# A token-major value projection ahead of the convolution, its first loads in pairs

## Chip, core and metric

The kernel runs on one core of a Trainium2 chip. The metric is the device time of the core in microseconds, from the start of the program to its end; lower is better.

## What is computed

Two transformer-like blocks on 512 tokens of width 1024, float32. Only the start of the first concerns the change:

```python
def first_block(x, norm_mix_g, w_in, ...):
    h = rms_norm(x, norm_mix_g[l])
    p = h @ w_in[l]
    q_a, k_a, v_a, o_a, i_a, f_a, q_b, k_b, v_b, g_a, g_b = jnp.split(p, split_idx, axis=-1)
    qk_a = jax.nn.silu(causal_conv(jnp.concatenate([q_a, k_a], axis=-1), conv_w[l]))
    ...
    h_a = mlstm_chunkwise(q_a..., k_a..., v_a..., i_pre, f_pre)
```

`rms_norm` divides each token's row by the root of its mean square and multiplies by a gain per column. After it come a mixer with decaying memory (the part "a"), a stick-breaking attention ("b"), gates, an output projection, a feed-forward part, and the second block with three attention branches.

## The kernel before, in words

The program is written by hand, engine by engine: each engine's list of instructions is in program order and semaphores join them. There is no scheduler. The order of the work is the order of the calls in the blocks `sync`, `tensor`, `scalar`, `vector` and `gpsimd`.

**Slabs.** Every projection is a sequence of weight slabs of 1 MB, numbered in the list `slabs` (lines 396 to 452): either 1024 rows by 256 columns ("narrow", 1 KB rows), or half the rows by 512 columns ("wide", 2 KB rows, two slabs for a full column block). The first are N_QA (four narrow slabs, kind "conv", for q_a and k_a), N_IF (one half-width slab, input and forget gates), N_VA (two column blocks, so four wide slabs, kind "va"), N_QB and so on. Slab n uses buffer n % 2 of `w_raw`, `w_hi`, `w_lo`. SP loads it (`load_slab`) once the split of the slab before it in that buffer is done. ACT rounds it (`split_hi`, L602), DVE takes the remainder (`split_lo`, L610), and TensorE makes three products for each tile and k: hi with hi, hi with lo, lo with hi (L633, and `mm_half`, L656, for wide slabs). The activations are split in the same way into `act_hi` and `act_lo`.

**Feature-major and token-major.** A "conv" or "if" tile has features on the partitions and all 512 tokens in the free dimension, so it needs all tokens' activations before its first product. A "va" tile has 128 tokens on the partitions and 512 columns: it needs only that block of 128 tokens. Each tile is 24 products of 128x128 by 512, into one PSUM bank. Feature-major tiles alternate between the two banks of `ps_g`; a wide block uses two banks of `ps_z` and both of `ps_g`.

**The start.** SP issues the four token blocks of x and some small vectors at once, then slab 0. ACT squares each block (L944), takes roots (L948), DVE scales each block into `xn` (L966), TensorE transposes `xn` 128 by 128 into eight banks (`feature_tiles`, L684), ACT and DVE split these into `act_hi` and `act_lo` with the gain as a per-partition scale (L741, L754). The small vectors, gain among them, are turned to columns by one transpose (L1091). Then come the products of slab N_QA.

**The convolution.** The evacuation of a conv tile is four DVE passes over the bank (L847, L850 three times), after which the bank is free; ACT applies Silu (L767). Between slab 0 and 1 TensorE makes the bias rows (L1102 to L1107), small products of a one-hot table for the second block, which DVE copies out (L1796). After the gate slab N_IF come, on ACT, three functions (L1509 to L1511) and, on DVE, a chain of seven operations on 8 rows (L1802 to L1815, called the gate chain here); both stand in the loop iteration n == N_VA, where DVE has no tile to evacuate. One more function, Exp (L1521), stands at n == N_VA + 2 on ACT.

## Time and profile before

| | us |
|---|---|
| median of 3 runs | 1359.02 (1358.73 to 1359.62) |
| profiled execution | 1358.28 |
| its span in the trace | 1356.6 |
| TensorE busy with products | 1314.5 (97% of the span) |
| DVE / ACT / GpSimd busy | 763.5 / 679.5 / 201.7 |
| mean granted TensorE clock | 0.994 |

The span is the time between the first and last event of the trace; the execution's own time is 1.7 us more. TensorE's busy time is modelled and overlaps at the joints, so single idle times are read from the rows of the timeline.

### The profile page before, as it was taken

The page shows a single profiled execution, that of the slowest core. Times are in us where ns is not written, and L with a number is a line of the kernel's source. Part 1 is how long each engine was busy: PE and PEld are TensorE (multiplying, and loading weights), DVE is VectorE, ACT ScalarE, POOL GpSimd, SP SyncE. Part 2 cuts the span into 40 slices and gives each one's busy share as a digit, 9 for nine tenths or more (in the row PEclk, how much of TensorE's full clock was granted, in tenths as well). Part 3 has the DMA queues.
Part 4 walks back from the last instruction along what each step waited for, and adds up shares of the span by engine and source line. Part 5 has one row for each costly group of instructions (what it writes and reads, how often), then busy time and mean ns, then how long its engine had stood idle before and what let it go on. Part 6 is the DMA issues. An engine that isn't in the chain of part 4 may idle for free.

```text
span 1356.6 us, 17827 instructions
## 1 busy us (share of the span) xinstructions
PE 1314.5 (97%) x7149; PEld 1098.8 (81%) x7149; DVE 763.5 (56%) x1217; ACT 679.5 (50%) x1053; POOL 201.7 (15%) x265
## 2 busy tenths in 40 slices
PE   6999999999999999999999999899999999999998
PEld 4887777787788887878878787788899998989876
DVE  4753444434544544595775858721266767776563
ACT  5244555347666424454635546445245667665232
POOL 1101332261000000000000000003612333331000
PEclk9999999999999999999999999999999999999999
DMA  8657443394435334134070420372612222222311
GB/s 172 103 121 115 73 85 70 88 205 113 62 63 62 81 106 159 59 114 135 1 236 12 154 95 1 93 221 78 139 38 72 71 71 71 69 94 66 108 63 62
DMA packets 94817, 128.97 MB, mean 95 GB/s; under 512 B 5839, under 2 KB 70463, under 8 KB 94736
## 3 DMA queue, kind: packets, MB, share of 16 engines
q1 hardware_dynamic: 88528, 108.70, 31.9%
q0 software_dynamic: 6064, 18.83, 5.3%
q8 instruction: 57, 0.93, 0.3%
q10 hardware_dynamic: 144, 0.31, 0.1%
q14 instruction: 24, 0.20, 0.0%
HBM read 124.94 MB, written 2.88 MB: 94 GB/s over the span
## 4 chain that ended last, share of the span: by engine, by line
PE 86%; DVE 7%; ACT 3%; DMA 2%; issue 2%; SPq 0%; POOL 0%; DVEq 0%; ACTq 0%
PE ps_g L633 44%; PE ps_g L656 8%; PE ps_z L656 8%; PE ps_t L1277 6%; PE ps_z L1388 3%; PE ps_z L1425 2%; PE ps_z L1277 2%; PE ps_t L1460 2%; DVE w_lo L610 2%; DMA w_raw<-in_w_in 2%; PE ps_t L1155 1%; ACT w_hi L602 1%; PE ps_t L1193 1%; PE ps_z L1207 1%; PE ps_t L1310 1%
## 5 line engine op out<-in xcount | busy, mean ns | idle before, releaser
L610 DVE TENSOR_TENSOR w_lo<-w_raw,w_hi 128x2048 fp32r<-128x2048 f32 (+1 forms) x84 | 193.5, 2304 | 233.0 <-ACT w_hi L602 233.0
L633 PE MATMUL ps_g<-act_hi,w_hi 128*128 128x512 f32 x784 | 310.3, 396 | 6.4 <-DVE act_lo L754 4.3
L633 PE MATMUL ps_g<-act_hi,w_lo 128*128 128x512 f32 x784 | 306.7, 391 | 0.0
L633 PE MATMUL ps_g<-act_lo,w_hi 128*128 128x512 f32 x784 | 306.5, 391 | 0.0
L602 ACT ACTIVATE w_hi<-w_raw 128x2048 fp32r<-128x2048 f32 (+1 forms) x84 | 159.2, 1895 | 113.3 <-PE ps_g L656 62.1
L633 PEld LDWEIGHTS ps_g<-act_hi,w_hi 128*128 128x128 f32 x784 | 148.0, 189 | 39.3 <-issue 5.0
L633 PEld LDWEIGHTS ps_g<-act_hi,w_lo 128*128 128x128 f32 x784 | 148.0, 189 | 31.5
L633 PEld LDWEIGHTS ps_g<-act_lo,w_hi 128*128 128x128 f32 x784 | 148.1, 189 | 29.7
L633 PE MATMUL ps_g<-w_hi,act_hi 128*128 128x256 f32 x320 | 93.4, 292 | 0.0
L633 PE MATMUL ps_g<-w_lo,act_hi 128*128 128x256 f32 x320 | 90.3, 282 | 0.0
L633 PE MATMUL ps_g<-w_hi,act_lo 128*128 128x256 f32 x320 | 90.2, 282 | 0.0
L2219 POOL TENSOR_SCALAR cmp_in_k<-pairk,vec 128x124 f32<-128x124 f32 x16 | 11.7, 744 | 503.3 <-ACT pairk L807 503.3
L1697 ACT ACTIVATE probs<-probs,rneg 128x128 f32<-128x128 f32 (+3 forms) x128 | 70.4, 551 | 12.3 <-DVE rneg L2041 10.8
L602 ACT ACTIVATE w_hi<-down_raw 128x2048 fp32r<-128x2048 f32 x24 | 46.0, 1918 | 57.5 <-PE ps_t L1277 35.8
L2239 POOL TENSOR_TENSOR q_parts<-qn,q_parts 64x512 fp32r<-64x512 f32 x32 | 41.9, 1310 | 140.7 <-ACT q_parts L1677 140.5
L633 PEld LDWEIGHTS ps_g<-w_hi,act_hi 128*128 128x128 f32 x320 | 61.1, 191 | 0.2 <-issue 0.2
L633 PEld LDWEIGHTS ps_g<-w_lo,act_hi 128*128 128x128 f32 x320 | 61.2, 191 | 0.0
L610 DVE TENSOR_TENSOR w_lo<-down_raw,w_hi 128x2048 fp32r<-128x2048 f32 x24 | 55.0, 2290 | 10.8 <-ACT w_hi L602 10.8
L633 PEld LDWEIGHTS ps_g<-w_hi,act_lo 128*128 128x128 f32 x320 | 61.0, 191 | 0.0
L2037 DVE CUSTOM_DVE_ANT_0 probs<-ps_z,tile_t 128x128 f32<-128x128 f32 (+3 forms) x128 | 54.9, 485 | 4.5 <-PE ps_z L1388 3.2
L789 ACT ACTIVATE ev_t<-ps_g 128x512 f32<-128x512 f32 x32 | 19.1, 596 | 74.9 <-PE ps_g L633 74.9
L656 PE MATMUL ps_g<-w_hi,act_hi 128*128 128x512 f32 x128 | 49.9, 390 | 0.7 <-DVE act_lo L752 0.7
(349 smaller groups left out, 2602.0 us busy)
## 6 DMA issues: line engine op xcount, KB each, us to landing
w_raw<-in_w_in SPq DMA_DIRECT2D x32, 1024.0 KB, 9.2
w_raw<-in_nsa_w_in SPq DMA_DIRECT2D x22, 1024.0 KB, 5.2
w_raw<-in_w_up SPq DMA_DIRECT2D x16, 1024.0 KB, 5.6
down_raw<-in_w_down SPq DMA_DIRECT2D x16, 1024.0 KB, 5.2
tile_t<-bias_rev_dram POOLq DMA_DIRECT2D x32, 256.0 KB, 3.1
bc<-stat_rows_dram POOLq DMA_DIRECT2D x24, 256.0 KB, 10.2
w_raw<-in_w_out SPq DMA_DIRECT2D x4, 1024.0 KB, 5.0
w_raw<-in_nsa_w_out SPq DMA_DIRECT2D x4, 1024.0 KB, 5.0
```

The source lines that it names most:

```text
L602: nc.scalar.activation(slab_view(w_hi[b], n), slab_view(raw(n), n), ACT.Copy).then_inc(hi_done, 1)
L610: nc.vector.tensor_tensor(slab_view(w_lo[b], n), slab_view(raw(n), n), slab_view(w_hi[b], n).bitcast(F32), ALU.subtract).then_inc(lo_done, 1)
L633: mm = nc.tensor.matmul(o, stationary, moving, start=(k == 0 and j == 0), stop=(k == KT - 1 and j == 2))
L656: mm = nc.tensor.matmul(bank(t), act[:, k, m], w[:, k - k0, :], start=(k == 0 and j == 0), stop=(k == KT - 1 and j == 2))
L789: nc.scalar.activation(ev_t[:, g, :], ps_g[:, g, :], ACT.Relu).then_inc(ev_act, 1)
L1277: mm = nc.tensor.matmul(down_bank(p, i), act[:, k, m], w[:, k, :], start=(first and k == 0 and j == 0), stop=(k == HALF_K - 1 and j == 2), ...
L1388: mm = nc.tensor.matmul(ps_z[:, at:at + w], q_parts[u % 2][:, b * P:(b + 1) * P], keys[u // 4 % 2][:, 0:w], start=(j == 0), stop=(j == 1))
L1425: mm = nc.tensor.matmul(ps_z[64 * e:64 * e + 64, CAUSAL + at * P:CAUSAL + (at + 1) * P], values[:, s, g * DH:(g + 1) * DH], probs_t[:, blo ...
L1460: mm = nc.tensor.transpose(ps_t[:, at:at + P], probs[u % 2][:, ROWS_AT[b] + s * P:ROWS_AT[b] + (s + 1) * P], ident)
L1697: ins = nc.scalar.activation(p, p, ACT.Exp, bias=rneg[:, u % 2, b:b + 1], accum_out=rsum[:, u % 2, b:b + 1])
L2037: ins = nc.vector.tensor_tensor_reduce(probs[u % 2][:, at:at + w], ps_z[:, at:at + w], tile_t[u % 2][:, S - w:S], 1.0, -3.0e38, ALU.add, A ...
L2239: nc.gpsimd.tensor_tensor(q_parts[u % 2][64 - half:128 - half, :], qn[half:half + 64, 4 * (h // 8) + h % 4, :], q_parts[u % 2][half:half + ...
```

## The change

The value projection is cut in two: its first column block becomes slabs 0 and 1 (N_VA), then come N_IF (slab 2), the four conv slabs N_QA (3 to 6) and the second column block N_VA2 (7 and 8). The first block's activations are made token block by token block: a gain row is loaded and spread over the partitions by two TensorE products into `ps_g` (two more into `ps_z` follow, whose result nobody reads), DVE scales and applies the gain in one operation, eight transposes of a token block go into two banks, and ACT and DVE split four tiles at a time (`first_high`, `first_low`). The transposes of the next token block stand between the third and fourth k of the current one. The first wide slab is split in two pieces, the second piece's remainder on GpSimd. SP issues x and the first slabs so that two loads are on their way at a time. The bias rows follow the value block, and their SBUF copies have a place of their own, so that the "if" evacuation no longer waits for their transfer. The gate chain moves from n == N_VA to n == N_QA, that is, between the first conv slab's evacuation and the second's, and ACT's Exp from n == N_VA + 2 to n == N_QA + 1. Semaphore counts and bank assignments follow. Nothing behind N_QB is changed.

```diff
-        bias_rev_sb = sb("bias_rev_sb", [HN, 640], at=t1 + 4096 + 4 * OH_W)
-        bias_fwd_sb = sb("bias_fwd_sb", [P, 8, HN], at=t1 + 4096 + 4 * OH_W + 2560)
+        bias_rev_sb = sb("bias_rev_sb", [HN, 640], at=arena + 4 * K16 + 4096)
+        bias_fwd_sb = sb("bias_fwd_sb", [P, 8, HN], at=arena + 4 * K16 + 4096 + 2560)
...
+        N_VA = add_wide("va", W, VA, 1)
+        N_IF = add("if", W, IF, 1, w=P)
         N_QA = add("conv", W, QA, 4)
-        N_IF = add("if", W, IF, 1, w=P)
-        N_VA = add_wide("va", W, VA, 2)
+        N_VA2 = add_wide("va", W, VA, 1, s0=1)
         N_QB = add("qb", W, QB, 8)
...
             elif kind == "if":
-
-                dve.wait_ge(bias_out, 32)
                 tile_done(dve, t)
...
-            for b in range(TB):
-                sp.dma_start(x_sb[:, b, :], x_rows[:, b, :]).then_inc(x_in[b], 16)
+            sp.dma_start(x_sb[:, 0, :], x_rows[:, 0, :]).then_inc(x_in[0], 16)
+            first_rows = W[0:HALF_K * P, VA:VA + WIDE].rearrange("(k p) n -> p k n", p=P)
+            sp.dma_start(first_pieces(w_raw[0], 0), first_rows[:, 0:2, :]).then_inc(first_w_in, 16)
+            sp.wait_ge(x_in[0], 16)
+            sp.dma_start(first_pieces(w_raw[0], 1), first_rows[:, 2:4, :]).then_inc(raw_landed[0], 16)
+            sp.wait_ge(first_w_in, 16)
+            sp.dma_start(x_sb[:, 1, :], x_rows[:, 1, :]).then_inc(x_in[1], 16)
+            sp.wait_ge(raw_landed[0], 16)
+            sp.dma_start(x_sb[:, 2, :], x_rows[:, 2, :]).then_inc(x_in[2], 16)
+            sp.wait_ge(x_in[1], 16)
+            sp.dma_start(x_sb[:, 3, :], x_rows[:, 3, :]).then_inc(x_in[3], 16)
+            sp.wait_ge(x_in[2], 16)
+            load_slab(1)
+            sp.wait_ge(x_in[3], 16)
...
-            for n in range(N_MLP):
-                if n == 1:
-                    sp.wait_ge(raw_landed[0], 16)
+            sp.wait_ge(first_w_lo, 1)
+            for n in range(2, N_MLP):
...
+            def first_turns(b):
+
+                pe.wait_ge(xn_ready, b + 1)
+                for j in range(2):
+                    if b >= 2:
+                        pe.wait_ge(first_lo, 2 * (b - 2) + j + 1)
+                    for k in range(4):
+                        mm = nc.tensor.transpose(first_bank(b, j)[:, k * P:(k + 1) * P],
+                                                 xn[b][:, (4 * j + k) * P:(4 * j + k + 1) * P], ident)
+                    mm.then_inc(first_t, 1)
+
+            pe.wait_ge(gain_row_in, 16)
+            pe.wait_ge(ones_set, 1)
+            for c in range(2):
+                mm = nc.tensor.matmul(ps_g[:, c, :], ones_row[0:1, 0:P], gain_row[:, c * 512:(c + 1) * 512],
+                                      start=True, stop=True)
+            mm.then_inc(gain_spread, 1)
+            for c in range(2):
+                nc.tensor.matmul(ps_z[:, 0:512], ones_row[0:1, 0:P], gain_row[:, c * 512:(c + 1) * 512],
+                                 start=True, stop=True)
+            pe.wait_ge(const_in, 16)
+            first_turns(0)
+            pe.wait_ge(first_w_lo, 1)
+            wh, wl = slab_view(w_hi[0], N_VA), slab_view(w_lo[0], N_VA)
+            for b in range(TB):
+                t, m = tile_of[N_VA] + b, slice(b * P, (b + 1) * P)
+                if b == 2:
+                    pe.wait_ge(xn_ready, TB)
+                pe.wait_ge(first_hi, 2 * b + 1)
+                for k in range(HALF_K):
+                    if k == 2:
+                        pe.wait_ge(lo_done, 1)
+                    nc.tensor.matmul(bank(t), act_hi[:, k, m], wh[:, k, :], start=(k == 0), stop=False)
+                    nc.tensor.matmul(bank(t), act_hi[:, k, m], wl[:, k, :], start=False, stop=False)
+                    if k == 0:
+                        pe.wait_ge(first_lo, 2 * b + 1)
+                    mm = nc.tensor.matmul(bank(t), act_lo[:, k, m], wh[:, k, :], start=False, stop=False)
+                    if k == 2 and b < TB - 1:
+                        first_turns(b + 1)
+            mm.then_inc(half_done, 1)
+            for b in range(TB):
+                pe.wait_ge(first_lo, 2 * b + 2)
+                mm_half(pe, N_VA + 1, b)
+            turn_vectors()
+            bias_rows()
+            mm_slab(pe, N_IF)
             for n in range(N_QA, N_QA + 4):
-                mm_slab(pe, n, activation_ready=features_ready(pe, n, 0) if n == N_QA else None)
...
-            mm_slab(pe, N_IF)
-            mm_slab(pe, N_VA)
-            mm_slab(pe, N_VA + 1)
-            mm_slab(pe, N_VA + 2)
+                mm_slab(pe, n)
...
+            act.wait_ge(ones_set, 1)
+            order.link(nc.scalar.activation(ssq[0:1, 0, 0:1], ones_row[0:1, 0:1], ACT.Sqrt))
...
+            first_squares(0)
+            first_root(0)
+            act.wait_ge(first_w_in, 16)
+            nc.scalar.copy(first_pieces(w_hi[0], 0), first_pieces(w_raw[0], 0)).then_inc(first_w_hi, 1)
+            act.wait_ge(raw_landed[0], 16)
+            nc.scalar.copy(first_pieces(w_hi[0], 1), first_pieces(w_raw[0], 1)).then_inc(hi_done, 1)
+            first_high(0, 0)
+            first_squares(1)
+            first_root(1)
+            first_high(0, 1)
+            first_squares(2)
+            first_root(2)
+            first_high(1, 0)
+            first_squares(3)
+            first_root(3)
+            first_high(1, 1)
+            first_high(2, 0)
+            split_hi(act, 1)
+            first_high(2, 1)
+            first_high(3, 0)
+            first_high(3, 1)
...
-            for n in range(N_QA, N_QB):
-                if n != N_IF:
+            for n in range(N_VA, N_QB):
+                if n not in (N_VA, N_IF):
                     split_hi(act, n + 1)
-                if n == N_VA:
+                if n == N_QA:
+                    act.wait_ge(vec_ready, 1)
...
-                    if n == N_IF - 1 and i == 1:
+                    if n == N_IF - 1 and i == TB - 1:
                         split_hi(act, N_IF + 1)
                     act_evacuate(act, n, i)
 
-                if n == N_VA + 1:
+                if n == N_VA2:
                     a_hi(0)
-                if n == N_VA + 2:
+                if n == N_QA + 1:
                     act.wait_ge(gate_dve, 1)
...
+            def first_normed(b):
+                dve.wait_ge(std_ready, b + 1)
+                r = rstd[:, 0, b:b + 1]
+                order.link(nc.vector.reciprocal(r, r))
+                if b == 0:
+                    dve.wait_ge(gain_spread, 1)
+                nc.vector.scalar_tensor_tensor(xn[b][:], x_sb[:, b, :], r, ps_g[:].rearrange("p a n -> p (a n)"),
+                                               ALU.mult, ALU.mult).then_inc(xn_ready, 1)
...
+            first_mean(0)
+            first_normed(0)
+            dve.wait_ge(first_w_hi, 1)
+            nc.vector.tensor_tensor(first_pieces(w_lo[0], 0), first_pieces(w_raw[0], 0),
+                                    first_pieces(w_hi[0], 0).bitcast(F32), ALU.subtract).then_inc(first_w_lo, 1)
+            first_low(0, 0)
+            first_mean(1)
+            first_normed(1)
+            first_low(0, 1)
+            first_mean(2)
+            first_low(1, 0)
+            first_normed(2)
+            first_mean(3)
+            first_low(1, 1)
+            first_normed(3)
+            first_low(2, 0)
+            first_low(2, 1)
+            first_low(3, 0)
+            dve.wait_ge(lo_done, 1)
+            split_lo(dve, 1)
+            first_low(3, 1)
+            split_lo(dve, N_IF)
...
+            split_lo(dve, N_IF + 1)
+            dve.wait_ge(oh_mm, 1)
+            nc.vector.tensor_copy(bias_rev_sb[:], ps_t[0:HN, 512:1152]).then_inc(oh_cp, 1)
+            nc.vector.tensor_copy(bias_fwd_sb[:], ps_t[:, 1152:1152 + 8 * HN]
+                                  .rearrange("p (c h) -> p c h", h=HN)).then_inc(oh_cp, 1)
...
-            for n in range(N_QA, N_QB):
-                split_lo(dve, n + 1)
+            for n in range(N_IF, N_QB):
+                if n != N_IF:
+                    split_lo(dve, n + 1)
                 for i in range(0 if k_half(n) == 0 else tiles_of(n)):
                     dve_evacuate(dve, order, n, i)
                 if n == N_QA:
-                    dve.wait_ge(oh_mm, 1)
-                    nc.vector.tensor_copy(bias_rev_sb[:], ps_t[0:HN, 512:1152]).then_inc(oh_cp, 1)
-                    nc.vector.tensor_copy(bias_fwd_sb[:], ps_t[:, 1152:1152 + 8 * HN]
-                                          .rearrange("p (c h) -> p c h", h=HN)).then_inc(oh_cp, 1)
-                if n == N_VA:
...
-                if n == N_VA + 1:
+                if n == N_VA2:
                     a_lo(0)
-                if n == N_VA + 2:
...
+            pool.wait_ge(hi_done, 1)
+            nc.gpsimd.tensor_tensor(first_pieces(w_lo[0], 1), first_pieces(w_raw[0], 1),
+                                    first_pieces(w_hi[0], 1).bitcast(F32), ALU.subtract).then_inc(lo_done, 1)
```

On DVE, at the end of the first conv slab and ahead of the second (`conv_t` is the convolution's result, `rows` the gates, `w_lo` the remainder of a slab), the changed kernel has:

```order
L862 SCALAR_TENSOR_TENSOR conv_t<-ps_g,vec,conv_t 128x509 [waits dve_order]
L1954 TENSOR_SCALAR rows_79<-rows_80 8x512 [waits gate_act,tile_free0]
L1955 TENSOR_TENSOR rows_79<-rows_79,rows_78 8x512 [waits dve_order]
L1957 SCALAR_TENSOR_TENSOR rows_80<-ones_row,rows_79 8x512 [waits dve_order]
L1960 TENSOR_TENSOR rows_81<-rows_81,rows_80 8x512 [waits dve_order]
L1964 SCALAR_TENSOR_TENSOR rows_78<-rows_81 8x512 [waits u_ready]
L1966 TENSOR_TENSOR rows_79<-rows_80,rows_78 8x512 [waits dve_order]
L1967 TENSOR_SCALAR rows_78<-rows_78 8x512
L622 TENSOR_TENSOR w_lo_57<-w_raw_53,w_hi_55 128x2048 [waits hi_done]
L859 TENSOR_SCALAR conv_t<-ps_g,vec 128x512 [waits ev_act,tile_ready]
```

The kernel before has at this place:

```order
L850 SCALAR_TENSOR_TENSOR conv_t<-ps_g,vec,conv_t 128x509 [waits dve_order]
L1796 COPY bias_rev_sb<-ps_t 16x640 [waits oh_mm]
L1797 COPY bias_fwd_sb<-ps_t 128x128
L610 TENSOR_TENSOR w_lo_56<-w_raw_52,w_hi_54 128x2048 [waits hi_done]
L847 TENSOR_SCALAR conv_t<-ps_g,vec 128x512 [waits ev_act,tile_ready]
```

The two bias copies have gone to an earlier place, and the seven operations on `rows` have come in ahead of the slab's remainder and the next tile.

On ACT, from the second conv slab's Silu to the third's, the changed kernel has:

```order
L779 ACTIVATE qk_a<-conv_t 128x512 [waits tile_free1]
L779 ACTIVATE qk_a<-conv_t 128x512 [waits tile_free0]
L1633 ACT_TABLE_LOAD
L1633 ACTIVATE rows_79<-rows_79 8x512 [waits gate_dve]
L614 ACTIVATE w_hi_54<-w_raw_52 128x2048 [waits tile_ready,raw_landed0]
L779 ACT_TABLE_LOAD
L779 ACTIVATE qk_a<-conv_t 128x512 [waits tile_free1]
```

The table load, the Exp and the reload for Silu now stand among the conv slabs; before, they stood between value slabs.

On TensorE, the changed kernel begins with:

```order
L1156 MATMUL ps_g<-gain_row,ones_row 128x512 [waits ones_set,gain_row_in]
L1156 MATMUL ps_g<-gain_row,ones_row 128x512
L1160 MATMUL ps_z<-gain_row,ones_row 128x512 x2
L1149 MATMUL ps_z<-cst,xn_58 128x128 [waits xn_ready,const_in]
L1149 MATMUL ps_z<-cst,xn_58 128x128 x3
L1149 MATMUL ps_t<-cst,xn_58 128x128 x4
L1174 MATMUL ps_z<-w_hi_54,act_hi 128x512 [waits first_hi,first_w_lo]
L1175 MATMUL ps_z<-w_lo_56,act_hi 128x512
L1178 MATMUL ps_z<-w_hi_54,act_lo 128x512 [waits first_lo]
```

Before, all 32 transposes and the vector transpose stood ahead of the first product.

## Rows read from the trace of the kernel before

**Rows 1.** The page: span, and the chain that ended last by engine.
```profile
span 1356.6 us, 17827 instructions
...
PE 86%; DVE 7%; ACT 3%; DMA 2%; issue 2%; SPq 0%; POOL 0%; DVEq 0%; ACTq 0%
```

**Rows 2.** Timeline of PE: start us, us, engine line op, count [idle before, releaser].
```profile
16.75 0.49 PE L684 MATMUL ps_z<-cst,xn 128*128 128x128 f32 x3
17.07 0.49 PE L684 MATMUL ps_t<-cst,xn 128*128 128x128 f32 x3
...
20.07 0.77 PE L633 MATMUL ps_g<-act_hi,w_hi 128*128 128x512 f32 x1 [2.50 <-DVE act_lo L754]
...
32.72 1.03 PE L1102 MATMUL ps_t<-onehot,table 33*16 33x512 f32 x2
33.59 0.38 PE L1104 MATMUL ps_t<-onehot,table 33*16 33x128 f32 x2
...
36.23 0.47 PE L633 MATMUL ps_g<-act_hi,w_hi 128*128 128x512 f32 x1 [0.39 <-DVE conv_t L850]
```

**Rows 3.** The chain that ended last, 0 to 150 us: start, us, what.
```profile
36.23 12.79 PE ps_g L633 x48
...
82.45 5.44 PE ps_g L656 x24
...
115.67 5.45 PE ps_g L656 x24
```

**Rows 4.** Loads: engine, op, count, KB each, median us from issue to landing.
```profile
x_sb<-in_x SPq DMA_DIRECT2D x1, 512.0 KB, 5.7
...
w_raw<-in_w_in SPq DMA_DIRECT2D x1, 1024.0 KB, 13.9
...
tile_t<-bias_rev_dram POOLq DMA_DIRECT2D x32, 256.0 KB, 3.1
...
vec_rows<-in_pos_v POOLq DMA_DIRECT2D x1, 8.0 KB, 5.1
...
m_rows_dram<-rows POOLq DMA_DIRECT2D x1, 16.0 KB, 2.7
```

**Rows 5.** Timeline of ACT: the first squares, and the Exp between value slabs.
```profile
5.52 1.06 ACT L944 ACTIVATE xn<-x_sb 128x1024 f32<-128x1024 f32 x1 [3.02 <-DMA x_sb<-in_x]
...
101.08 1.92 ACT L602 ACTIVATE w_hi<-w_raw 128x2048 fp32r<-128x2048 f32 x1
103.01 1.28 ACT L1521 ACT_TABLE_LOAD   x1
104.31 0.63 ACT L1521 ACTIVATE rows<-rows 8x512 f32<-8x512 f32 x1
```

**Rows 6.** Timeline of DVE and POOL: operations whose like the change adds.
```profile
64.68 1.23 DVE L610 TENSOR_TENSOR w_lo<-w_raw,w_hi 128x1024 fp32r<-128x1024 f32 x1 [1.65 <-ACT w_hi L602]
...
126.87 1.49 DVE L1827 SCALAR_TENSOR_TENSOR decay<-ps_z,decay 128x1280 f32<-128x1280 f32 x1 [1.00 <-POOL decay L2124]
...
128.44 1.49 POOL L2166 TENSOR_TENSOR den_sum<-decay 128x384 f32<-128x384 f32 x1 [1.18 <-DVE decay L1827]
```

**Rows 7.** Timeline of DVE: a conv tile's first pass, the last pass, the gate chain's first and last.
```profile
49.05 0.75 DVE L847 TENSOR_SCALAR conv_t<-ps_g,vec 128x512 f32<-128x512 f32 x1 [2.15 <-PE ps_g L633]
49.84 2.32 DVE L850 SCALAR_TENSOR_TENSOR conv_t<-ps_g,vec,conv_t 128x511 f32<-128x511 f32 x3
...
83.23 0.41 DVE L1802 TENSOR_SCALAR rows<-rows 8x512 f32<-8x512 f32 x1 [2.18 <-ACT rows L1511]
...
88.21 0.41 DVE L1815 TENSOR_SCALAR rows<-rows 8x512 f32<-8x512 f32 x1
```

**Rows 8.** Stretches: us, PE, PEld, DVE, ACT, POOL busy, granted clock, DMA share, GB/s.
```profile
20.00:22.00 2.00, 1.93 (x5) 1.57 (x6) 2.00 (x4) 1.64 (x3) 0.00 (x0) 0.50 0.93 90
...
532.00:533.00 1.00, 1.00 (x6) 1.00 (x7) 1.00 (x3) 0.20 (x1) 0.00 (x0) 0.50 1.04 408
...
536.00:537.00 1.00, 1.00 (x12) 1.00 (x10) 0.00 (x0) 0.47 (x1) 0.00 (x0) 1.00 1.04 383
```

103 lines of the change are left out of this document (65 added, 38 removed).

## The prediction

> **What bounds the kernel now.** The page comes first: of the 1356.6 us, TensorE holds 86% of the chain that ended last [rows 1]. So a change at the start pays only if TensorE gets through its work earlier, and whatever delays it later in the same stage is to be set against that. Behind the value slabs nothing is changed, so I compare one event: the end of the last value tile. In the chain it is 115.67 + 5.45 = 121.12 us [rows 3]. The rest, 121.12 to 1356.6, I carry over as it is: slabs 9 and 10 keep their numbers and their buffers, and the `u` transposes and the load of the decay rows still stand one value slab, 10.9 us, ahead of that event.
>
> The timeline of TensorE shows how it comes to 121.12. The first product starts at 20.07 [rows 2]. A tile of 24 products takes 5.44 [rows 3], 0.227 each. There are 17 tiles (8 conv, 1 gate, 8 value, a wide tile counted whole): 17 x 5.44 = 92.5. The bias rows take from 32.72 to 35.84, 3.1, and a wait for a conv bank follows, 0.39 to 36.23 [rows 2]. Then 48 products take 12.79 instead of 10.88 [rows 3], 1.9 lost; the first 48 took 32.72 - 20.07 = 12.65 [rows 2], 1.8 lost, where the granted clock stood at 0.50 from 20 us on, the lower level of 1.2 GHz [rows 8]. Sum: 20.07 + 92.5 + 3.1 + 0.4 + 1.9 + 1.8 + 0.3 for the `u` transposes = 120.1, and a remainder of 1.0 in joints between tiles, which I keep for the new order.
>
> **The change part by part.**
>
> *First product, -9.1.* x block 0 still lands at 5.5 [rows 5]. The next 512 KB came 1.4 later (issued at 1.2, 5.7 to landing [rows 4]); that place is now the first piece of weights, 6.9. The second piece is issued at 5.5. For one 512 KB load with a neighbour the nearest rows are 3.1 (256 KB) and 5.7 (512 KB, queued) [rows 4]; I take 3.7, nearer to the first, since at most one other load is ahead: 9.2. The same step gives blocks 1, 2, 3 at 10.6, 13.0, 14.3. Squares end at 6.7 (1.06 and a read-out), mean, root and reciprocal 0.6 (the table is loaded beforehand), and the scaling by row and gain from PSUM about 1.2, from 1.49 for 1280 columns [rows 6]: `xn` at 8.6. Eight transposes are 0.107 each at full clock (3 in 0.32, [rows 2]) and twice that at half: done by 10.3. ACT rounds the second weight piece from 9.3 to 10.3, then the first four transposed tiles, and the first product starts at 11.0, 9.1 before 20.07.
>
> The gain row goes first in ACT's queue and costs nothing only if it lands early: two spreading products of 512 columns in plain float32 took 0.87 each at full clock (32.72 to 33.59, [rows 2]), so 3.5 at half, and two more that nobody reads follow. Issued at about 0.8, it lands between 2.7 (16 KB on a quiet queue) and 5.1 (the small loads of the start) later [rows 4]; I take the lower end, 3.5, since nothing is ahead of it.
>
> *The four token blocks, +4.8.* I laid the new lists of ACT, DVE and TensorE side by side, with squares 1.2, a rounding of four tiles 0.6, a remainder 0.7, the scaling 1.25. GpSimd's half of the split is 1024 columns; its 384 took 1.49 [rows 6], so I take 3.1: ready at 13.5, just when the third k needs it. The blocks start at 11.0, 17.2, 21.7 and 25.7, the last ends at 28.4. Of these 17.4 us 10.9 are the 48 products, 3.6 the 24 transposes of blocks 1 to 3, which now stand between products, 1.8 the half clock up to about 16 (a choice: as much as before), and 1.1 waits, the longest for all four `xn` ahead of block 2 (0.8). Before, the first 48 products and their half clock took 12.65. So 4.8 come back. DVE's split of slab 1 (2.3, ready at 28.1) is just in time.
>
> *Behind them, +0.4.* The second half of the value block is 10.9, to 39.3. The vector transpose, formerly in TensorE's idle time, is now on the path, 0.4. The bias rows and the half clock behind them are the same 3.1 and 1.9 as before. The gate tile ends at 50.1. The load of slab 3 starts when slab 1 is split, at 28.1, with slab 4's behind it; such a pair took 13.9 [rows 4]: 42.0, rounded and split by 46.2, needed at 50.1. It is covered by 3.9. Dropping the wait for the bias transfer and moving the bias copies cost nothing: DVE idles there.
>
> *The convolution, +4.4.* This is the term that I rest most on. Call the end of the gate tile T. Conv tiles 0 to 3 end at T+5.4, +10.9, +16.3, +21.8 if no bank holds them. DVE needs 3.1 for a tile (49.05 to 52.16, [rows 7]), so tile 1 is out at T+14.0. Then the gate chain runs, 83.23 to 88.62, 5.4 [rows 7]; before it stood where DVE had no tile. Then comes the remainder of slab 5, 2.3: T+21.7, in time. But tile 2, ready since T+16.3, is out only at T+24.8, and tile 4 wants its bank at T+21.8: **3.0 of waiting**. Next, ACT's Silu of tile 3 ends at T+28.5, then table and Exp take 1.9 (1.28 + 0.63) and the rounding of slab 6 another 1.9 [rows 5]; its remainder on DVE follows at T+32.4 to 34.7, ahead of tile 4, which is out at T+37.8 where tile 6 wants its bank at T+35.7: **2.0 more**. Against 5.0, the kernel before had 0.6 (0.39 in rows 2, the rest at slab 3's start). A half clock behind the first wait would slow tiles 4 and 5 by 1.7, but only eats the second wait: T+37.8 is set by DVE and ACT. Conv ends at T+48.7 = 98.8.
>
> *Value slabs 7 and 8*: 21.8 and 0.3, unchanged.
>
> Sum: -9.1 + 4.8 + 0.4 + 4.4 = **+0.5** on the profiled execution, 1358.28: 1358.8. The median of the runs shown is 0.7 above that execution, so **1359.5**. A measurement of this kernel can tell about 0.2%, 2.7 us, from no change: this is the same.
>
> **What the Trainium skill says against it.** First the rows: at 532 us, with transposes alone running, the granted clock was 0.50, and 4 us later, with nothing but transposes between, it was 1.00 [rows 8]. So transposes brought it back here. "TensorE: Matmul & The Clock Gate", Part 4, says that transposes do not count as busy for the clock; the trace speaks against it. By that rule the interleaved blocks would stay at half clock (the third rival). "DMA: Bandwidth & Descriptors", Anatomy of one DMA, gives about 2 us plus the bytes at 436 GB/s, 3.2 for 512 KB where I took 3.7; the first product would then start 0.5 earlier and the sum be 0.0.
>
> **The rivals.**
>
> 1. *Faster: the blocks run without waits.* If loads land a microsecond earlier and the clock is up from the first product, it starts at 10.4 and the stage is 10.9 + 24 x 0.107 = 13.5 plus some waits, 14.2, to 24.6 instead of 28.4: -3.8, 1355.7. For it: in the first microseconds the transposes of the kernel before wait only on DVE. Against: the chain squares, root, scaling, transposes, rounding, remainder is about 5 us per token block, and DVE and ACT carry near 3 each.
> 2. *Slower: the gain row comes late.* Small loads at the start took 5.1 [rows 4]. Landing at 5.9, spreading ends at 9.4, the two idle products at 12.7 at half clock, and the first product starts at about 14.5: +3.5, 1363.0. The place is TensorE ahead of the first transposes. It decides from a landing of about 3: at half clock the four products take 7.0 and the first transposes 0.9, and ACT is free to round at 10.4. Each later microsecond costs one.
> 3. *Slower: half clock through all four blocks*: 48 x 0.2 more for the products, less the waits they fill, 5.8 by the same laying-out: 1365.3.
> 4. *The stalls in the convolution do not come*, because DVE's chain runs in gaps I do not see. That would be -5.0, 1354.5. Against: the lists are in program order, and every duration is a row.
>
> **How the numbers follow.** My forecast, within 2.7 us of no change: 0.60. Rival 1: 0.14, rival 4: 0.03, so faster 0.17. Rival 2: 0.13, rival 3: 0.05, and 0.05 for small delays together (loads, a stretch of half clock more), so slower 0.23. The range 1355.8 to 1363.2 reaches to rivals 1 and 2 and leaves out about one in ten on either side: below, the parts of rival 1 past its price and rival 4; above, rival 3 and the far end of rival 2. It takes in the price of a load pair between 3.1 and 5.7 (-0.6 to +2) and of the gain row.
>
> **What would show it right or wrong.** In the changed profile: the first product near 11; four groups of 12 products with eight transposes between them, ending near 28; the gate tile's end near 50; then exactly two waits of TensorE for `conv_t`, near 3.0 and at most 2.0, before the third and the fourth conv slab; the last value tile's end between 119 and 124. The forecast is wrong if TensorE's wait for the gain row or `xn` is longer than 10, if the clock is 0.50 after 20 us, if the waits for `conv_t` sum to under 3, or if the stretch behind the last value tile is not the old 1235.5.

## The result, and the profile after

The changed kernel takes **1362.38 us**, the median of 20 runs (1359.32 to 1365.16), beside 1358.57 for the kernel before in as many (1356.58 to 1360.19). The ratio is 1.0030, with a 95% interval of 1.0024 to 1.0036: slower by about 4 us. The forecast was 1359.5 and no difference; the time lies inside its range, and the side is the one that had a chance of 0.23. The profiled execution took 1362.75 us.

The page of the changed kernel, against [rows 1]:
```profile
span 1361.0 us, 17862 instructions
...
PE 83%; DVE 9%; ACT 3%; issue 2%; DMA 2%; POOL 1%; SPq 0%; DVEq 0%; ACTq 0%
```
TensorE's share of the chain fell by three points; DVE took two and GpSimd one. Where DVE holds the chain is the convolution, as foreseen.

**The start.** Timeline of TensorE, changed kernel:
```profile
9.33 1.11 PE L1149 MATMUL ps_z<-cst,xn 128*128 128x128 f32 x4
10.23 1.06 PE L1149 MATMUL ps_t<-cst,xn 128*128 128x128 f32 x4
13.75 0.76 PE L1174 MATMUL ps_z<-w_hi,act_hi 128*128 128x512 f32 x1 [2.46 <-ACT act_hi L1579]
...
16.02 0.63 PE L1178 MATMUL ps_z<-w_hi,act_lo 128*128 128x512 f32 x1
16.45 0.53 PE L1174 MATMUL ps_z<-w_hi,act_hi 128*128 128x512 f32 x1
...
17.65 1.09 PE L1149 MATMUL ps_t<-cst,xn 128*128 128x128 f32 x8 [0.22 <-DVE xn L1891]
```
and of ScalarE in the same time:
```profile
8.17 1.04 ACT L1585 CAST w_hi<-w_raw 128x1024 fp32r<-128x1024 f32 x1 [1.99 <-DMA w_raw<-in_w_in]
12.08 1.04 ACT L1587 CAST w_hi<-w_raw 128x1024 fp32r<-128x1024 f32 x1 [2.87 <-DMA w_raw<-in_w_in]
13.03 0.58 ACT L1579 CAST act_hi<-ps_z 128x512 fp32r<-128x512 f32 x1
14.51 1.06 ACT L1570 ACTIVATE xn<-x_sb 128x1024 f32<-128x1024 f32 x1 [0.90 <-DMA x_sb<-in_x]
```
The second weight piece lands at 12.1 where I had 9.2, the next `x` tile at 14.5 where I had 10.6. The rounding of the first turned tiles stands behind the piece on ScalarE, so the first product starts at 13.75 and not at 11.0. The four blocks then take 17.0 us (to 30.75), as laid out (17.4).

**The convolution.** Waits of TensorE, 40 to 130 us (in total, times, longest); then the timelines of DVE, with the gate chain's first and last, and of ScalarE, with the Exp:
```profile
PE ps_g L645 <- DVE conv_t L862: 3.2, 2, 2.9
PE ps_t L1231 <- DVE decay L1978: 1.7, 1, 1.7
```
```profile
64.59 0.41 DVE L1954 TENSOR_SCALAR rows<-rows 8x512 f32<-8x512 f32 x1
...
69.57 0.41 DVE L1967 TENSOR_SCALAR rows<-rows 8x512 f32<-8x512 f32 x1
```
```profile
78.88 1.28 ACT L1633 ACT_TABLE_LOAD   x1
80.17 0.63 ACT L1633 ACTIVATE rows<-rows 8x512 f32<-8x512 f32 x1
80.71 1.90 ACT L614 ACTIVATE w_hi<-w_raw 128x2048 fp32r<-128x2048 f32 x1
82.63 1.28 ACT L779 ACT_TABLE_LOAD   x1
```
The two waits are there, 2.9 and 0.3. The chain that ended last gives the end of the last value tile, 116.12 + 5.45 = 121.57, against 121.12 [rows 3]: +0.45, forecast +0.5.
```profile
88.09 11.12 PE ps_g L645 x48
...
116.12 5.45 PE ps_g L668 x24
```

**Behind it**, where I carried everything over, the time is 4 us longer. First the table: at 82.63 the rows above show ScalarE loading Silu's table *behind* the Exp. So the Exp of the first decay, which found its table in place before (last loaded at 103.01 [rows 5]), must load it again, on the path. Timeline of ScalarE and of TensorE:
```profile
122.08 1.92 ACT L614 ACTIVATE w_hi<-w_raw 128x2048 fp32r<-128x2048 f32 x1
124.01 1.28 ACT L1653 ACT_TABLE_LOAD   x1
125.31 1.93 ACT L1653 ACTIVATE decay<-m_bc,u_col 128x512 f32<-128x512 f32 x4
```
```profile
130.00 1.45 PE L1231 MATMUL ps_t<-decay,v_a 128*128 128x512 f32 x3 [1.71 <-DVE decay L1978]
```
In the kernel before this product started at 128.41 with a wait of 0.57. The changed kernel is now 1.59 behind. Second, the clock. Stretches of TensorE (us, busy, granted clock, DMA share, GB/s), changed kernel and then the kernel before:
```profile
74.00:76.00 2.00, 0.67 (x2) 0.69 0.96 213
76.00:78.00 2.00, 2.00 (x6) 0.50 0.67 258
...
310.00:312.00 2.00, 1.68 (x7) 0.57 0.85 190
312.00:314.00 2.00, 2.00 (x12) 0.58 0.31 109
```
```profile
310.00:312.00 2.00, 2.00 (x15) 1.00 0.48 178
```
Half clock at the first stick-breaking head makes it 3.1 behind. Third, near 1079 us DVE stands still for 1.41 us with no releaser that the profile shows, in a loop that the change does not touch:
```profile
1079.33 0.29 DVE L2188 CUSTOM_DVE_ANT_0 probs<-ps_z,tile_t 128x128 f32<-128x128 f32 x1 [1.41 <-issue]
```
That makes it 4.5. Which of these three belong to the change was the first question.

### The profile page after: what moved, and what is told of

The parts are those of the page before. It is cut to its first block, busy times and chain, and to the rows that moved or that the text cites. A ratio compares the mean times of both kernels' runs of the same rounds, so it can differ in the third digit from the quotient of the medians.

```text
span 1361.0 us, 17862 instructions
## 1 busy us (share of the span) xinstructions
PE 1321.4 (97%) x7157; PEld 1100.1 (81%) x7157; DVE 765.6 (56%) x1219; ACT 681.3 (50%) x1057; POOL 200.2 (15%) x266
## 4 chain that ended last, share of the span: by engine, by line
PE 83%; DVE 9%; ACT 3%; issue 2%; DMA 2%; POOL 1%; SPq 0%; DVEq 0%; ACTq 0%
PE ps_g L645 43%; PE ps_g L668 7%; PE ps_z L668 7%; PE ps_t L1353 6%; PE ps_z L1353 2%; PE ps_z L1464 2%; PE ps_z L1501 2%; DVE w_lo L622 2%; PE ps_t L1536 2%; PE ps_t L1231 1%; PE ps_t L1269 1%; PE ps_z L1283 1%; PE ps_t L1386 1%; ACT w_hi L614 1%; PE ps_z L1307 1%
## 5 line engine op out<-in xcount | busy, mean ns | idle before, releaser
L645 PEld LDWEIGHTS ps_g<-act_hi,w_hi 128*128 128x128 f32 x784 | 147.6, 188 | 39.3 <-issue 7.9
L1846 ACT COPY probs_t<-ps_t 128x512 f32<-128x512 f32 x32 | 18.8, 587 | 60.0 <-PE ps_t L1536 60.0
```

The costliest lines, as they stand in the source:

```text
L645: mm = nc.tensor.matmul(o, stationary, moving, start=(k == 0 and j == 0), stop=(k == KT - 1 and j == 2))
```

## The experiments

A ratio below is to the kernel before on the same chip, with its 95% interval. "Lost to half clock" is worked out from windows of 2 us: busy time of TensorE times (1 - granted clock). "Offset" is how far one event lies behind the same event in the first trace of the kernel before. The medians of the changed kernel and of the kernel before in the result were taken beside each other, those of the experiments beside other runs of the kernel before (medians 1357.79 to 1358.17), so a difference of less than about 1 us between an experiment's median and 1362.38 says little; the ratios are the safer comparison.

### Four first edits

`e_exp`, the Exp back behind head 0's casts:
```diff
-                if n == N_QA + 1:
+                if n == N_VA2:
                     act.wait_ge(gate_dve, 1)
                     nc.scalar.activation(rows[1][:], rows[1][:], ACT.Exp, ...)
```


> The changed kernel with one edit: ScalarE's Exp of the gate rows stands after the query casts of head 0, as in the kernel before, so no Silu follows it. Theory A (the time is lost in separate pieces, and one is the Exp table that ScalarE now loads ahead of the first decay, 1.28 us at 124.01): no table load between the last w_hi copy and decay, TensorE's wait for decay 0.4 to 0.6 instead of 1.7, offset to the kernel before at that point +0.3 to +0.5 instead of +1.59, and the time 1.1 to 1.4 us below the changed kernel's 1362.4, so about 1361.1. Theory B (the later losses, half clock at 310 us and idle stretches at 1078 and 1229 us, only follow from the shifted time): it falls by 3 us or more, to 1359 or less. Theory C (the table is hidden, or the gain is given back in a later wait): no change, 1362.4.

Measured: 1361.44 (11 runs), ratio 1.0023 (1.0013 to 1.0032). The table load ahead of the decay is gone and the wait is the old one:
```profile
127.74 1.45 PE L1231 MATMUL ps_t<-decay,v_a 128*128 128x512 f32 x3 [0.58 <-DVE decay L1978]
```
In the trace that is theory A. The times do not show it by themselves: the median is 0.9 below the changed kernel's, but the two ratios' intervals overlap (the changed kernel's is 1.0024 to 1.0036). This trace has no granted clock of 0.50 ahead of 500 us, and its span is 3.7 shorter than the changed kernel's, which looks like B; the traced execution is the second fastest of the eleven, and the median does not bear B out.

`e_gate`, the same and DVE's gate chain behind the last conv tiles:
```diff
-                if n == N_QA:
+                if n == N_QA + 3:
                     wait_tile_free(dve, tile_of[N_IF])
                     dve.wait_ge(gate_act, 1)
```


> As the run before, and VectorE's chain of seven gate-row steps (5.3 us) moved from behind the first two convolution tiles to behind the last two. Theory A (the chain delays the convolution, and TensorE waits for conv_t): the two waits for conv_t (2.9 and 0.3 us) are gone, the last value tile ends 3.0 to 3.2 us earlier (about 118.4 against 121.57 in the changed kernel and 121.12 in the kernel before), no new wait for the gate columns because the chain ends near 104.5 and TensorE turns them near 107; with the table load gone too, the time is 4.1 to 4.5 us below the changed kernel, about 1358.1, which is level with the kernel before. Rival: the gain row's chain becomes late instead (memory round trip of m_rows to m_bc), so that decay or the first head waits, and the time stays within 1 us of the run before.

Measured: 1360.27 (11 runs), ratio 1.0018 (1.0009 to 1.0027), 2.1 below the changed kernel. No wait for `conv_t` is left, and the last value tile ends 2.85 us earlier. But 2.1 of that is given back: the wait for the decay grows from 0.58 in `e_exp` to 2.71. The size is the rival's; the mechanism is mostly another.
```profile
128.16 1.12 PE L1231 MATMUL ps_t<-decay,v_a 128*128 128x512 f32 x2 [2.71 <-DVE decay L1978]
```
ScalarE shows what came last:
```profile
121.36 1.92 ACT L614 ACTIVATE w_hi<-w_raw 128x2048 fp32r<-128x2048 f32 x1 [2.03 <-DMA w_raw<-in_w_in]
123.19 1.90 ACT L1653 ACTIVATE decay<-m_bc,u_col 128x512 f32<-128x512 f32 x4
```
It stands idle for 2.03 until the 1 MB slab lands that it has to round ahead of the decay, and the decay follows the rounding without a gap. The broadcast of the decay rows, loaded at the same time (issued at 108.17, 14.4 to landing as the median of three), is there near 122.6, some 0.6 before the decay starts: late as well, but not last.

`e_loads`, the opening without waits on SyncE:
```diff
-            sp.wait_ge(x_in[0], 16)
             sp.dma_start(first_pieces(w_raw[0], 1), ...)
-            sp.wait_ge(first_w_in, 16)
             sp.dma_start(x_sb[:, 1, :], ...)
...
```


> The changed kernel with the six waits taken out of SyncE's opening, so that the tiles of x, both pieces of the first slab and slab 1 are issued one behind another. Theory A (loading two at a time costs the start): x tile 1 lands by 9 us instead of 14.48, weight piece 1 by 9 instead of 12.06, the first product starts at 10.5 to 11.5 instead of 13.75, the four blocks end at 28 to 29 instead of 30.91, and the time falls by 2 to 3 us, to about 1360. Rival B (the first tile and first piece come later, since everything shares the rings, and the clock at the start is half for as many products anyway): first product at 13 or later, and the time within 0.7 us of the changed kernel. Rival C: the gain at the start is real but given back in the wait for conv_t or in a later load (slab 2), so the last value tile ends within 0.7 us of 121.57.

Measured: 1364.30 (5 runs), ratio 1.0043 (1.0030 to 1.0055); A is refuted. Whether it is slower than the changed kernel the times leave open, since the intervals overlap. The second weight piece is issued at 1.69 instead of 4.54 and lands at 11.5 instead of 12.1; `x` tile 1 is issued at 2.19 and is there by 13.1. The first product moves from 13.75 to 13.21. **Taking turns is not what sets the start**; the loads slow each other either way: over the first 10 us the DMA engines are busy 0.84 of the time and move 187 GB/s (0.85 and 185 in the changed kernel). Of the gain of 0.5 only 0.2 is left at the end of the four blocks (30.56 for 30.75), since they wait for `xn` as before. Its trace is 2.3 us further behind at head 0's values than the changed kernel's, and there it has lost 3.4 more to half clock, most of it behind the same wait of 2.9 for `conv_t`:
```profile
76.00:78.00 2.00, 1.28 (x3) 0.50 0.98 285
78.00:80.00 2.00, 2.00 (x6) 0.50 0.34 130
80.00:82.00 2.00, 2.00 (x7) 0.50 0.00 0
```

`e_table`, on the kernel *before*, a reader-less Silu behind its Exp:
```diff
                     nc.scalar.activation(rows[1][:], rows[1][:], ACT.Exp, ...)
+                    order.link(nc.scalar.activation(ssq[0:1, 0, 0:1], ones_row[0:1, 0:1], ACT.Silu))
```


> The kernel before with one instruction added: a one-element Silu on ScalarE behind the Exp of the gate rows, with no reader, so that the Exp table has to be loaded again ahead of the first decay. Nothing else of the change is in it. Theory A: one more table load of 1.28 us on the path to decay, TensorE's wait there longer by 1.1 to 1.3, and the time 1.1 to 1.3 us above the kernel before (1358.6), about 1359.8. Theory B (a shift of about 1 us there by itself brings half clock at 310 us and the idle stretches in the last part): 2.5 us or more above, 1361 or more. Theory C: less than 0.4 us above.

Measured: 1359.86 (11 runs), ratio 1.0008 (0.9999 to 1.0017), that is -0.1 to 2.3 us: B is out, while the time alone cannot tell A from C. The trace agrees with A in place and size:
```profile
122.59 1.28 ACT L1542 ACT_TABLE_LOAD   x1
```
```profile
128.56 1.77 PE L1155 MATMUL ps_t<-decay,v_a 128*128 128x512 f32 x4 [1.70 <-DVE decay L1828]
```
The wait grows from 0.57 to 1.70, that is 1.13. "ScalarE activation tables: per-element evaluation and per-set limits" of the Trainium skill, section "What a function is on this engine", puts functions of different sets one table load apart, and 1.28 is what every such row here shows.

### Two repeats, the repair, and an earlier first product

`before_again` and `after_again` are the two kernels, unchanged.

> The kernel before, unchanged, for a second trace. Theory A (stretches of half clock of about 1.6 us each come behind idle waits of TensorE, at some of the places where they can come and not in every run): half clock again at 532 to 536 and 872 to 878 us, and at a part of 20 to 24, 36 to 42 and 308 to 316 us; with the same places as in the first trace (20 to 24 and 36 to 42) the offset to it is 0 to 0.3 throughout, otherwise it moves by 1.5 to 1.7 at each place that differs. Theory B (the places are fixed by the program): exactly the four places of the first trace.

> The changed kernel, unchanged, for a second trace. Theory A: the first product again at 13.6 to 13.9, the wait for conv_t again 2.8 to 3.0, the wait for decay again 1.7, since these come from the order of the work; half clock at a part of 44 to 50, 74 to 84 and 308 to 316 us, each worth 1.3 to 3 us, not necessarily the two (74 to 80, 310 to 314) of the first trace. Theory B: exactly the places of the first trace, so that a loss of 1.5 us at the first stick-breaking head belongs to the change.

`before_again` took 1359.19, `after_again` 1363.20. B falls in both: the repeat of the kernel before has half clock at 308 to 312, where its first trace had none, and none at 20 to 24:
```profile
308.00:310.00 2.00, 1.94 (x10) 0.66 0.99 292
310.00:312.00 2.00, 2.00 (x10) 0.50 0.56 188
```
So the 1.5 us at the first stick-breaking head are no cost of the change. The missing stretch at 20 to 24 bears on the gain of the new start:
```profile
30.62 1.03 PE L1102 MATMUL ps_t<-onehot,table 33*16 33x512 f32 x2
...
35.62 0.77 PE L633 MATMUL ps_g<-act_hi,w_hi 128*128 128x512 f32 x1 [1.87 <-DVE conv_t L850]
```
Here the kernel before has its first 48 products behind it at 30.62 and not at 32.72, but waits 1.87 for `conv_t` behind the bias rows where the first trace waited 0.39 [rows 2], and goes on at 35.62 for 36.23. `e_table` and `e_before_head` start alike and go on at 35.33. So of the 2.1 us at the start only 0.6 to 0.9 reaches the work behind the bias rows. What the new start gains is best counted there. The changed kernel has 48 products more behind it at that point, 10.88 us, so the gain is 36.23 + 10.88 - 44.92 = 2.2 between the first traces and 35.62 + 10.88 - 44.20 = 2.3 between the repeats. The forecast puts that point at 39.3 + 0.4 + 3.1 = 42.8, a gain of 4.3.

The repeat of the changed kernel has half clock at 44 to 48, behind the bias rows, where I had put it, and none at 74 to 80; its waits for `conv_t` are 4.5 in total instead of 3.2.

`e_best`: Exp as in `e_exp`, the gate chain in two parts, the first broadcast early, head 0's next slab split behind the decay:
```diff
                         .then_inc(u_ready, 1)
+                if n == N_QA + 1:
                     dve.wait_ge(u_ready, 1)
...
-            pool.wait_ge(u_t, 1)
             load_m(0)
+            pool.wait_ge(u_t, 1)
             load_m(1)
...
                 n = N_QB + h
-                split_hi(act, n + 1)
+                if h:
+                    split_hi(act, n + 1)
...
                 ins.then_inc(a_decay, 1)
+                if h == 0:
+                    split_hi(act, n + 1)
```
(and so on DVE for `split_lo`, behind the decay's multiply).

> The changed kernel with five moves: ScalarE's Exp of the gate rows behind the casts of head 0; VectorE's chain of gate rows cut in two, 3.0 us behind the first convolution slab and 2.3 us behind the second; the first broadcast m_bc issued without waiting for TensorE's turn of the gate columns; and in head 0 the split of the next slab behind the decay instead of ahead of it, on both engines. Theory A (what the change loses before 130 us is waits, which are order alone): waits for conv_t together under 0.8 us, the last value tile ends near 118.7, decay starts near 119.5 and TensorE does not wait for it, so the first product of head 0's values starts near 125.5 (128.41 before, 130.00 in the changed kernel); the time is 1.5 to 3.5 us below the kernel before, about 1355.5. Rival: the slab whose split was moved (w_hi, w_lo of the second head) becomes late and TensorE waits for it 1.5 us or more, and the time is level with the kernel before.

Measured: 1356.66 (11 runs), ratio 0.9991 (0.9982 to 1.0000). Every step is in place: one wait for `conv_t`, 0.6; decay at 119.42, right behind the last value copy; none for the decay:
```profile
119.42 1.92 ACT L1654 ACTIVATE decay<-m_bc,u_col 128x512 f32<-128x512 f32 x4
121.25 1.90 ACT L614 ACTIVATE w_hi<-w_raw 128x2048 fp32r<-128x2048 f32 x1
```
```profile
125.47 1.88 PE L1231 MATMUL ps_t<-decay,v_a 128*128 128x512 f32 x5
```
That is 5.7 us below the changed kernel's median (5.3 by the ratios), more than all that it lost. It moves five things at once, so it shows that the loss was order, not how much each move brings.

`e_high`, the first turned tiles rounded ahead of the second weight piece:
```diff
+            first_high(0, 0)
             act.wait_ge(raw_landed[0], 16)
             nc.scalar.copy(first_pieces(w_hi[0], 1), ...)
-            first_high(0, 0)
```


> The changed kernel with one edit: ScalarE makes the high part of the first four turned tiles before it waits for the second weight piece, not behind it. Theory A (the first product is late because this part stands behind the piece that lands at 12.06): the first product starts at 10.9 to 11.3 instead of 13.75, near my forecast. The block work behind it is bound by the second piece's low part (ends 15.5) and x tile 1 (lands 14.48), so the end of the four blocks moves by 0.9 us at most and the time by 0 to 1 us. Rival: the early start brings the whole 2.6 us, and the blocks end at 28.3 to 28.6; then my forecast erred by the order on ScalarE and not by the loads.

Measured: 1365.37 (5 runs), ratio 1.0048 (1.0035 to 1.0060), slower than either theory said. In the trace A's steps nearly hold:
```profile
11.80 0.77 PE L1174 MATMUL ps_z<-w_hi,act_hi 128*128 128x512 f32 x1
...
15.11 0.50 PE L1174 MATMUL ps_z<-w_hi,act_hi 128*128 128x512 f32 x1 [0.58 <-POOL w_lo L2287]
...
16.68 1.10 PE L1149 MATMUL ps_t<-cst,xn 128*128 128x128 f32 x8 [0.59 <-DVE xn L1891]
```
The first product is 1.95 earlier, at 11.80 where A had 10.9 to 11.3, because the gain row landed at 2.80 and not at 2.21; the end of the blocks is 0.98 earlier (29.77). But the mean granted clock of its five runs is 0.990 to 0.993, against 0.992 to 0.998 in the changed kernel's twenty.

### The last four

`e_high_again` repeats it, `e_best_again` repeats the repair, `e_nowarm` drops the two products of the gain row that nothing reads, and `e_before_head` puts two of `e_best`'s moves, the early broadcast and the split behind the decay, into the kernel before:
```diff
             mm.then_inc(gain_spread, 1)
-            for c in range(2):
-                nc.tensor.matmul(ps_z[:, 0:512], ones_row[0:1, 0:P], ...)
```


> The kernel of e_high, unchanged, for a second trace: its first product came early and its time was still 3 us above the changed kernel, with a mean granted clock of 0.990 to 0.993 against 0.992 to 0.998. Theory A (an earlier first product followed by waits makes stretches of half clock more frequent, and these are the loss): three or more stretches ahead of 320 us, worth 5 us or more together, and the same waits as in its first trace. Theory B (the loss is a wait that the first trace missed): a wait of 1 us or more that neither its first trace nor the changed kernel has.

Measured: 1364.86, one run. Mostly theory A: half clock at 16 to 22, 44 to 52, 78 to 82 and 312 to 318, with 6.6 us lost ahead of 128 us, and its waits for `conv_t` and for the decay are the changed kernel's:
```profile
46.00:48.00 2.00, 2.00 (x6) 0.50 0.30 73
48.00:50.00 2.00, 2.00 (x7) 0.50 0.87 134
```
One wait is longer than in the first trace, 1.55 for 0.58, and the changed kernel has none at this place; the half clock at 16 to 22 comes right behind it:
```profile
15.53 0.50 PE L1174 MATMUL ps_z<-w_hi,act_hi 128*128 128x512 f32 x1 [1.55 <-POOL w_lo L2287]
```
An earlier first product only makes TensorE wait for GpSimd's remainder of the second piece. Why this order draws more half clock further on stays open.

> The kernel of e_best, unchanged, for more runs and a second trace, beside the next kernel. Theory A: the order of the work gives the same offsets again (wait for conv_t under 0.8 us, first product of head 0's values 3 us earlier than in the kernel before where the same stretches of half clock fall), the median 1 to 2 us below the kernel before. Rival: the first result was chance, and it is within 0.5 us of the kernel before.

Measured: 1357.73 (11 runs), ratio 0.9993 (0.9983 to 1.0002). The offsets came again (first product of head 0's values 3.3 us earlier), the gain in time did not fully: the median is 1.2 us below the kernel before the first time and 0.4 this time, at the edge of what can be told.

> The kernel before with only those of the five moves that need nothing of the change: the first broadcast m_bc issued without waiting for the turned gate columns, and in head 0 the split of the next slab behind the decay. Theory A (e_best gains by the token-major start, once its waits are gone, and by these moves only what the wait for decay was worth, 0.57 us): the wait at the first product of head 0's values is gone, 0.4 to 0.6 us below the kernel before, about 1357.4, and 0.5 to 1.5 us above e_best. Rival: the gain of e_best is all from these moves, and the two are equal.

Measured: 1356.75 (11 runs), ratio 0.9989 (0.9980 to 0.9998), 1.0 below the repaired change beside it and 0.1 above its first result. Of all experiments only its interval lies below 1. The two moves give the kernel before about 1.5 us (0.3 to 2.7 by that interval), so as much of the 5.3 that the repair gave the changed kernel was never the change's loss; the 3.8 left fit what it had lost. So the rival holds as far as the times can tell: **freed of its waits, the token-major start is worth nothing measurable over the old start with the same two moves.** By its traces `e_best` was 2.5 to 2.8 ahead at head 0's values, of which 1.2 is half clock that fell in the trace of `e_before_head` and not in those of `e_best`; that trace (1359.48) is also the slowest of its eleven runs. Where the times lose the rest is open.

> The changed kernel without its two products of the gain row that nothing reads. Theory A (they cost nothing and bring nothing, since the first product waits for the weight piece that lands at 12): the first turned tiles come at 7.8 instead of 9.33, the first product still at 13.0 to 13.8, the products up to 16.4 at the same pace, and the time within 0.7 us of the changed kernel. Theory B (they keep TensorE's clock up): the products of the first blocks run at 0.427 us each beyond 18 us, and the time is 1 to 3 us higher.

Measured: 1364.02 (5 runs), ratio 1.0041 (1.0028 to 1.0055). Turned tiles at 7.71, first product at 13.41, as A had it; nine products and not six run at the slow pace, to 17.39. That is not the missing products' doing: with them in, nine run slowly in `after_again`, `e_exp`, `e_loads` and `e_best` too, in `e_exp` to 17.98. So B's sign is not there. The median is 1.6 above the changed kernel's with overlapping intervals, and with five runs the time is left undecided.

### The traces side by side

For each trace: the offset of head 0's first value product (128.41 in the kernel before), what half clock took ahead of it and around 310 us, and the growth of the offset from 1060 to 1250 us.

```
kernel          offset   lost <128   lost ~310   1060-1250   span
before            0         3.3         0           0        1356.6
before_again     -0.68      1.5         1.7         1.39     1357.5
e_table           0.15      1.5         3.0         0.56     1358.7
e_before_head    -0.43      2.9         3.2         0.19     1357.8
after             1.59      1.3         1.6         1.22     1361.0
after_again       2.48      1.7         3.0         0.97     1361.5
e_exp            -0.67      0           0           1.04     1357.3
e_gate           -0.25      1.7         0          -0.44     1356.1
e_loads           3.93      4.7         0           1.10     1361.7
e_high            2.28      3.2         1.5         0.87     1361.3
e_high_again      4.58      6.6         1.7         1.85     1363.1
e_nowarm          3.30      3.1         1.7         0.71     1362.3
e_best           -2.94      1.7         3.0         0.94     1356.0
e_best_again     -3.27      1.7         0           0.99     1354.5
```

Offset less what half clock took is what the order of the work costs: -3.3 and -2.2 for the kernel before, +0.3 and +0.8 for the changed one. The distance is 2.5 to 4.1 us, and the medians differ by 3.8. The order's cost contains the slow products at the very start of the changed kernel's traces, five to nine with 0.2 us lost on each, since the granted clock reads 1.00 there.

The columns do not add up to the differences in span: half clock falls differently at two more places, 520 to 600 us (the offset drops there by 1.1 to 1.4 in `after_again`, `e_table`, `e_before_head` and `e_best`) and 800 to 900 us (by 1.7 in `before_again` and `e_high_again`). And a traced execution is one of many: those of `e_exp`, `e_gate` and `e_high` are 2.3 to 2.4 us below their medians, that of `e_before_head` 2.7 above.

## Why the prediction was right or wrong

The range held and the likeliest case did not. By its steps:

- **First product, 11.0: wrong, 13.75.** The failed number is the price of a load beside others. I took 3.7 us for 512 KB, nearer to a row of 256 KB (3.1) than to the one of 512 KB (5.7); the second piece took 7.5, from 4.54 to 12.1, past the far end of my bounds. My other estimate, 3.2, is farther off still. `e_loads` shows that waiting in turns was not the reason. The gain row landed at 2.21 where I had 3.5; the second rival did not come.
- **The gain of the new start behind the bias rows, 4.3: wrong in size, 2.2.** It follows from the first product: the 2.75 us came through, less 0.4 in the blocks and 0.2 behind them. The repeats give 2.3.
- **Four blocks, 17.4: right, 17.0**, though not part by part: the transposes took 2.4 where I had 3.6 (24 x 0.107, from my own row, is 2.6). The clock stood at 1.00 through the interleaved transposes, at 0.227 a product from 17 us on, so the third rival fell. "TensorE: Matmul & The Clock Gate" of the Trainium skill, Part 4: PE-mode transpose, has transposes not counting as busy; with eight of them to every twelve products nothing of that was seen here, and of the ten traces only `e_high_again` has half clock inside the blocks, behind its wait.
- **Half clock behind the bias rows, 1.9: right in kind.** It is absent from the changed kernel's first trace and there in eight of the ten traces of its family (the two of the changed kernel and the eight of its variants), 1.7 us as a rule.
- **Waits for `conv_t`, 3.0 + 2.0: right.** 2.9 + 0.3 with 1.3 lost to half clock behind the first, and 4.5 without it in the repeat. That a half clock there "only eats the second wait" is what these two show.
- **Sum at the last value tile, +0.5: +0.45, by luck.** The late start (+2.75) met an absent half clock (-1.9), less half clock at the start and smaller waits. And the trace of before that I set it against carried 3.3 us of half clock; its repeat ends this tile 0.68 sooner, that of the changed kernel 0.91 later. Between the repeats the difference is 2.0, not 0.5: 2.3 gained at the start against 4.5 of waits. So half of the loss stands ahead of the last value tile.
- **"The rest, 121.12 to 1356.6, I carry over as it is": wrong, 1239.4 for 1235.5.** One of my own signs of being wrong came true. Between the repeats it is 1239.0 for 1237.1, 2.0 more: the other half of the loss. I named slabs, buffers, the `u` transposes and the decay rows as unchanged, and forgot the state of ScalarE: which table is loaded. The Exp moved ahead of Silu, so the first decay pays 1.28, of which 1.1 reaches TensorE (`e_table`, and `e_exp` the other way). The price stood in [rows 5]; I had even counted it where it was moved to. That is 1.1 of the 3.8 us.
- The other parts of the stretch behind: half clock at 310 us is not the change's. A stand of DVE without a releaser between 1060 and 1100 us (in `e_best_again` one of TensorE), which costs 0.7 to 1.5, is in all ten traces of the changed family and in none of the four of the kernel before. But two of those have one of 1.1 to 1.2 at 1103 to 1105 us, and later ones bring the growth up to 1.39. On the mean of 1060 to 1250 the family stands 0.93 behind and the others 0.54: some 0.4 that I did not foresee, and whose cause is open.

## What to carry to other kernels

When work is moved, list what each engine has *set up* for the next stage, not only its queue: a table-bound function moved ahead of another kind leaves a table load to the next one of its own, which may stand on the path. Compare more than one trace of the same kernel before trusting a difference of 2 us at some point: here half clock alone moved a trace by 0 to 6.6 us in the first 128. Half clock ahead of a wait costs only what the wait would not have taken: the 2.1 us at the start of the kernel before shortened its wait for `conv_t` by 1.5. And a wait that is removed pays only as far as the next thing due lets it; of 2.85 us freed ahead of the first head, 2.1 were taken by a slab that landed late and was rounded ahead of the decay, with a broadcast just before it, until the split went behind the decay and the broadcast no longer waited.

## What the runs showed of the hardware that I had not expected

**Half clock comes behind idle stretches of TensorE, but not each time, and not only there.** Behind the same wait of 2.9 us for `conv_t` it was absent in two traces of the changed kernel's order (`e_exp`, `after_again`), cost 1.3 to 1.6 in four, and 3.0 in `e_loads`. "TensorE: Matmul & The Clock Gate" of the Trainium skill, section "HAM oscillation — how this bites in real kernels", has a wait between groups of matmuls bring the clock down; the traces agree, with this spread. But at 44 to 50 us the half clock came in eight of ten traces with no wait ahead of it: there TensorE had been busy for 3.1 us with the small products of the bias rows.

**At the very start the pace is half while the granted clock reads 1.00.** In the changed kernel six products from 13.75 to 16.4 take 0.427 us each, which is what the products of the kernel before took at a granted 0.50 (21.06 to 22.77 us), and from 17 us on 0.227. Yet the column reads 1.00 in both stretches; the slow one:
```profile
14.00:16.00 2.00, 2.00 (x5) 1.00 0.83 252
```
At the start the pace of the products is the better reading.

**Opening loads are slow in either way of issuing them that was tried.** The same half megabyte took 7.5 us to land (4.54 to 12.1) with one other load of SyncE at a time beside it, and 9.8 (1.69 to 11.5) issued at once, behind two loads and ahead of four; ScalarE and GpSimd loaded tables of 298 and 214 KB meanwhile in both.
